# A hybrid decoder block with a mixture of experts on one core: row places copied ahead of gathers, second rows turned after unit 14, records' places ahead of two splits

## The reference, cut to what matters

```python
logits = hf @ w_router + b_router
top_vals, top_idx = lax.top_k(logits, TOP_K)            # 4 of 32
gates = softmax(top_vals)
# tokens sorted by expert, each expert's rows padded to blocks of 128
def expert_block(xb, e):
    gu = xb @ w_gate_up[e] + b_gate_up[e]               # 1024 -> 2048
    gate, up = gu[:, :1024], gu[:, 1024:]
    gate = minimum(gate, 7.0); up = clip(up, -7.0, 7.0)
    act = (up + 1) * (gate * sigmoid(1.702 * gate))
    return act @ w_down[e] + b_down[e]                  # 1024 -> 1024
out = segment_sum(ys[dest] * gate_of_row, token_of_row) + x
```

## Time and profile before

| what | value |
|---|---|
| median of 3 runs | 1645.24 us |
| profiled execution | 1642.67 us |
| its span | 1640.8 us |
| PE busy | 1605.7 us, 98% of the span |
| DVE busy | 1343.3 us, 82% |
| ACT busy | 1051.9 us, 64% |
| POOL busy | 436.4 us, 27% |
| mean granted clock of PE | 0.990 |

### The profile page before, as it was taken

How to read it: one execution, slowest core, us unless ns; L and a number is a source line. 1 busy time by engine, 2 the same in 40 slices (tenths; PEclk the granted TensorE clock), 3 DMA queues, 4 the chain that set the end, 5 groups by cost and what they waited for, 6 DMA issues and landing times.

```text
span 1640.8 us, 24160 instructions
## 1 busy us (share of the span) xinstructions
PE 1605.7 (98%) x7853; PEld 1319.3 (80%) x7853; DVE 1343.3 (82%) x1050; ACT 1051.9 (64%) x912; POOL 436.4 (27%) x287
## 2 busy tenths in 40 slices
PE   8999999999998989999999999999999999999997
PEld 6797777788896768888888888888888888888885
DVE  6974555523658879999999999999999999999995
ACT  5533444422346667777877777777787777777874
POOL 0000000501103643343422234232343323333230
PEclk8999999999999999999999999999999999999999
DMA  7331222333367889999999999999999999999993
GB/s 246 116 103 52 77 77 77 114 99 109 125 250 275 338 307 379 365 379 387 388 383 370 379 391 387 379 376 377 386 389 381 376 379 384 386 386 377 373 377 124
DMA packets 117210, 476.92 MB, mean 291 GB/s; under 512 B 17005, under 2 KB 60249, under 8 KB 67879
## 3 DMA queue, kind: packets, MB, share of 16 engines
q1 hardware_dynamic: 104612, 456.59, 73.3%
q0 software_dynamic: 12560, 19.81, 4.8%
HBM read 469.78 MB, written 23.83 MB: 301 GB/s over the span
## 4 chain that ended last, share of the span: by engine, by line
PE 93%; DVE 4%; issue 1%; ACT 1%; DMA 0%; POOLq 0%; ACTq 0%; SPq 0%; DVEq 0%
PE ps L657 29%; PE ps L659 29%; PE ps L658 29%; PE ps L897 2%; DVE work L1471 2%; PE ps L766 1%; PE ps L786 1%; PE ps L775 1%; PE ps L926 1%; PE ps L932 0%; DVE zT L1347 0%; DMA r<-in_x 0%; DVE r L1479 0%; PE ps L846 0%; DVE w_lo L1347 0%
## 5 line engine op out<-in xcount | busy, mean ns | idle before, releaser
L1347 DVE TENSOR_TENSOR zT<-raw,zT 128x2048 fp32r<-128x2048 f32 x96 | 217.6, 2295 | 52.3 <-ACT zT L1020 52.3
L1788 POOL DMA_INDIRECT r<-expert_inputs_by_quarter,quarter_at x124 | 215.1, 1734 | 52.7 <-issue 28.6
L1347 DVE TENSOR_TENSOR w_lo<-more_raw,w_hi 128x2048 fp32r<-128x2048 f32 x96 | 217.6, 2294 | 4.0 <-ACT w_hi L1020 2.1
L1347 DVE TENSOR_TENSOR zT<-more_raw,zT 128x2048 fp32r<-128x2048 f32 x96 | 219.9, 2292 | 1.1 <-ACT zT L1020 1.1
L1020 ACT ACTIVATE w_hi<-raw 128x2048 fp32r<-128x2048 f32 x96 | 184.4, 1922 | 52.4 <-PE ps L659 42.3
L1347 DVE TENSOR_TENSOR w_lo<-raw,w_hi 128x2048 fp32r<-128x2048 f32 x96 | 215.8, 2274 | 1.1 <-issue 1.0
L657 PE MATMUL ps<-zT,xT 128*128 128x512 f32 x512 | 203.6, 398 | 3.8 <-DVE zT L1347 3.8
L657 PE MATMUL ps<-w_hi,xT 128*128 128x512 f32 x512 | 201.3, 393 | 5.4 <-DVE xT L1664 2.7
L1020 ACT ACTIVATE zT<-more_raw 128x2048 fp32r<-128x2048 f32 x96 | 184.2, 1919 | 34.0 <-PE ps L659 30.4
L659 PE MATMUL ps<-zT,xT 128*128 128x512 f32 x512 | 200.2, 391 | 0.0
L658 PE MATMUL ps<-zT,xT 128*128 128x512 f32 x512 | 200.2, 391 | 0.0
(11 more groups left out here) (275 smaller groups left out, 3166.2 us busy)
## 6 DMA issues: line engine op xcount, KB each, us to landing
more_raw<-in_w_gate_up SPq DMA_DIRECT2D x129, 1024.0 KB
raw<-in_w_gate_up SPq DMA_DIRECT2D x127, 1024.0 KB
raw<-in_w_down SPq DMA_DIRECT2D x65, 1024.0 KB
more_raw<-in_w_down SPq DMA_DIRECT2D x63, 1024.0 KB
raw<-in_w_in SPq DMA_DIRECT2D x29, 1024.0 KB, 5.3
r<-in_x SPq DMA_DIRECT2D x8, 512.0 KB, 6.3
raw<-in_w_branch_conv SPq DMA_DIRECT2D x4, 1024.0 KB, 5.0
raw<-in_w_out SPq DMA_DIRECT2D x4, 1024.0 KB, 4.9
```

The source lines that it names most:

```text
L1347: nc.vector.tensor_tensor(expert_pair(1, c), chunk, expert_pair(0, c).bitcast(F32), ALU.subtract).then_inc(split_lo, 2)
L1788: nc.gpsimd.indirect_dma_start(out=quarters[:, part, :], out_offset=None, in_=h2_quarters, in_offset=bass.IndirectOffsetOnAxis(ap=quarter_ ...
```

## The change

Three edits. On VectorE, `block_offsets` moves ahead of the reading of the first rows, and `place_records` and `gates` ahead of the splits of chunks 2 and 3. On PE, half 1 of the second rows is turned after unit 14 instead of after unit 15, and the wait for its copy moves from ahead of the loop to unit 8 in every round; ScalarE's copies of the second rows get a wait for the units that read the old rows. On GpSimd, the copy to `uix` becomes a function of its own, `row_column`, which each round calls ahead of `gather_next`.

```diff
@@ PE @@
                 if j == 10:
                     second_rows(0)
-            second_rows(1)
-            pe.wait_ge(turned_read, SECOND_ROWS)
+                if j == 14:
+                    second_rows(1)
+            pe.wait_ge(turned_read, SECOND_ROWS - 1)
             with pe.Fori(1, nblk) as g:
...
+                    if j == 8:
+                        pe.wait_ge(turned_read, SECOND_ROWS)
                     gate_up(g, j)
@@ ScalarE @@
             def second_rows(half):
                 sc.wait_ge(turned_pe, FIRST_ROWS + half + 1)
+                sc.wait_ge(used, unit_base(0) + 8 * half + 8)
@@ VectorE @@
+            block_offsets()
             for half in range(2):
...
+            place_records()
+            gates()
             split_expert(0, 2)
             split_expert(0, 3)
-            block_offsets()
-            place_records()
-            gates()
@@ GpSimd @@
-            def scatter(g, earlier, outputs):
+            def row_column(g, earlier):
                 gp.wait_ge(y_ok, earlier)
                 nc.gpsimd.tensor_copy(uix[:, 1:3], ...).then_inc(row_column_ok, 1)
+            def scatter(g, outputs):
                 gp.wait_ge(y_ok, outputs)
...
                 g = before + 1
+                row_column(g, 2 * before)
                 gather_next(g)
-                scatter(g, 2 * before, 2 * before + 2)
+                scatter(g, 2 * before + 2)
                 stored(before)
```

More of the change, by code:

```diff
@@ L1904, in _ @@
                 turn_round(before)
-            scatter(nblk, 2 * but_one, 2 * nblk)
+            row_column(nblk, 2 * but_one)
+            scatter(nblk, 2 * nblk)
             stored(but_one)
-            scatter(nblk + 1, 2 * nblk, 2 * nblk + 2)
+            row_column(nblk + 1, 2 * nblk)
+            scatter(nblk + 1, 2 * nblk + 2)
 INS = ["x", "norm1_g", "w_in", "q_norm_g", "k_norm_g", "rel_bias", "conv_w", "w_branch_conv", "w_branch_attn",
```

## The result

| | before | after |
|---|---|---|
| median of 5 runs each, us | 1645.24 | 1632.64 (1631.41 to 1635.9) |
| profiled execution, us | 1642.67 | 1631.41 |
| its span, us | 1640.8 | 1629.4 |

The ratio of after to before is 0.9936, with a 95% interval of 0.9922 to 0.9949: about 10.5 us. (It is not the quotient of the two medians above, which is 0.9923.) The same kernel timed twice more gave 0.9943 (0.9931 to 0.9955) and 0.9940 (0.9927 to 0.9953), which is 9.4 and 9.8 us, so some 10 us is what the change is worth. The predicted 13.6 us was too much, though the predicted 1631.6 us lies 1 us from the median.

The account below looks back on a forecast made before the run. PE (TensorE) was taken to bound the kernel, with only its four waits and slow-clock stretches to win. -1.85 - 4.0 - 7.8 = -13.6 us from the median 1645.24 gave 1631.6 us, range 1629 to 1636.5.

Parts of the forecast that it names:

- Part 1: First expert, unit 8: moving the records' places ahead of two VectorE splits removes PE's wait, -1.85 us.
- the cover: First expert: chunks 2 and 3 are ready 0.8 and 1.3 us before PE wants units 4 and 6.
- the register load: VectorE, first expert: 0.96 us counted ahead of chunk 4's split, which then starts at 517.6.
- Part 2: Loop start: turning the second rows after unit 14 removes PE's wait and slow clock, -4.0 us in sum.
- the wait for the clamps: Unit 1 of the loop: new PE wait for the first expert's clamped up half, +0.4 us, 0 to 1 possible.
- Part 3: Second round: copying output rows' places ahead of the gathers shortens PE's stop, -9.5 + 1.7 = -7.8 us.
- I take 5.6: Second round: GpSimd's lead taken as 5.6 us, between 3.8 and 7.3, so unit 4 waits 1.55 us.
- run in step with VectorE: GpSimd's last records lie beside the same splits as before, 6 us earlier; the reason given for a lead near the middle.
- the first rival: GpSimd's chain doesn't keep up: lead 3.5 us, unit 4 waits 3.7, clock falls, 4.2 us less gained, 1635.8; chance 12%.
- The blocked copy: Second round: a VectorE split could shut out GpSimd's moved copy, turning the 1.7 us into about 3.9; left out.
- The copy as cause: Second round: the store waits for GpSimd's copy; the rival that it doesn't gave 1639.4, chance 5%.
- The weights' stream: Steady rounds, rival: weight loading becomes the bound, 0.5 us in each of 30 rounds, 1646.6; chance 5%.

Follow-up runs that it names:

- part 1 alone: Only VectorE's edit (block_offsets, place_records and gates moved ahead), against the kernel before: ratio 0.9993 (0.9984 to 1.0001).
- part 2 alone: Only PE's edit (second rows turned after unit 14, with its moved waits), against the kernel before: ratio 1.0015 (1.0005 to 1.0025).
- part 3 alone: Only GpSimd's edit (copy to `uix` ahead of the gathers), against the kernel before: ratio 0.9963 (0.9951 to 0.9975).
- beside part 2: PE's and GpSimd's edits together, without VectorE's, against the kernel before: ratio 0.9968 (0.9958 to 0.9979).
- the earlier copy: Changed kernel with the first `uix` copy directly behind the slots' landing, ahead of four loads and the index computation: ratio to before 0.9929, again 0.9931.

## Why the prediction was right in time and wrong in a term

- **Part 1, at unit 8: right.** Predicted -1.85 us, 2.0 us in the trace of part 1 alone. block_offsets lay in the idle time. Chunk 2's split began at 510.49, which counted from the first expert's matmul is 1.3 us later than before (1.5 predicted), and the cover held: no wait at unit 4. Chunk 4's split began directly behind chunk 3's, without the 0.96 us put down for the register load.
- **Part 2: right.** Predicted -4.0 us, -3.9 us with part 2 alone; the wait for the clamps was 0.16 us printed and the clock stayed at 1.00. The stretch from the first expert to round 1, which holds parts 1 and 2, came out at -6.0 us for the predicted -5.85.
- **Part 3: right mechanism, wrong size.** The step that failed is "I take 5.6" for GpSimd's lead. Counted from the first expert's matmul, the moved copy could have run at 575.8 - 509.05 = 66.75 us before; it ran at 62.95 after, a lead of 3.8 us (4.6 and 3.5 us in the other two traces). Unit 4 so waited 3.4 us (2.6 and 3.8), not 1.55, and a half-speed stretch from 576.7 to 580.1 came with it, 1.7 us more. Together that is 3.6 of the 3.8 us by which round 2 to 3 missed its -7.8. The working had a range for the lead, 3.8 to 7.3 us, and took a value near its middle; the three traces lie at 4.6, 3.8 and 3.5 us, at its lower end. Where the lead went, by the same count: 4.1 us at the first gather (record 8 took 2.88 us), 5.0 at the last gather's end, 3.5 at the last record's end (records 9 to 11 took 1.92, 0.98 and 2.46 us, before 1.02, 0.98 and 0.97; record 12 gave 1.1 us back), 2.8 when the loads had landed, 3.8 after the index computation. I had argued that the records "run in step with VectorE" and so keep the lead; they lose 1.5 us of it, for the gathers' earlier end lets records 9 and 11 meet splits that they had missed. The landings add scatter: in the three traces of the changed kernel the last record ends within 0.04 us of the same point, and the index computation starts 61.5 to 62.6 us behind the first expert's matmul.
- What happened is in its size the first rival, GpSimd's chain falling behind: a lead of 3.5 us, a wait of 3.7 us, a clock lost, 9.4 us in all. It had 12%, and the forecast 72%. That the median of 1632.6 us lies nearer to the forecast than to that rival's 1635.8 is luck in the base: the ratios say 9.4 to 10.5 us, while the two medians differ by 12.6. The base of 1645.24 us was high; in the four later comparisons the kernel before had medians of 1641.4 to 1643.0 us, and the changed kernel 1631.4 and 1631.7.
- **The blocked copy.** I left the Trainium skill's rule (SBUF — State Buffer, Who interferes with whom), that a VectorE instruction with two SBUF inputs contends with a GpSimd one that reads SBUF, out of the sum for this place. The rows agree with it: the copy took 0.19 us with VectorE idle and 2.26 us beside a split, the index computation 0.60 us and 3.90 us. It didn't strike the copy in the changed kernel. What was lengthened instead were the issues of the records, and for these the rows alone speak: 0.96 to 1.03 us clear of splits or where one began behind them, 1.9 to 3.1 us beside them.
- The copy as cause was shown, not only argued: moving it alone takes 6.2 us off the second round (part 3 alone), the profile of after names it, beside part 2 it takes off 4.6 us there, and the earlier copy leaves 0.6 us of the stop. The weights' stream didn't become the bound: the steady round shown is 34.44 us at a DMA share of 0.99 as before, and the mean over 28 rounds was 34.39, 34.46 and 34.49 us in three traces, 34.42 before.

## What to carry to other kernels

When two chains meet, price a change by both arrival times: the gain of one part is capped by the lead of the other chain, and parts measured alone (0.9993, 1.0015, 0.9963, product 0.9971) don't give their sum (0.994). Work that GpSimd does beside VectorE's float32 splits had no fixed price here (a record's issue took 1 to 3 us), so a lead on GpSimd's queue should be carried as a range of several microseconds and not as a shifted copy of the old times. And when a stop is removed, ask who used it: here the stop was the time in which GpSimd ran unhindered.

## What the runs showed of the hardware

An index computation of 128x192 elements on GpSimd took 0.60 to 0.63 us in the seven traces where it met no split, and 1.45 to 4.02 us in the seven where it met one or more splits of 2.28 us. VectorE was slowed as well: between 585 and 605 us one split took 2.75 to 3.09 us instead of 2.28 in eleven traces, each time beside the same GpSimd operation, a TENSOR_TENSOR that took 1.0 to 2.8 us. Between 510 and 620 us of the fourteen traces, idle times of PE of up to 2.4 us had no half-speed stretch, one of 2.4 and one of 1.6 us a few microseconds apart included; those of 2.6 us and more all had one, which began within them or behind them. The half-speed stretch at 503 us, in a part with many short pauses of PE, was there in nine of the fourteen traces and missing in five, of one and the same kernel too; the first expert starts at 508.8 to 510.7 us where it is there and at 507.6 to 507.7 us in three of the five without it, so it moves a trace by 1 us and more; the other two without it start at 509.0 and 509.3.
